# Stacking the high and low token parts into one 512-column product in the feed forward layers of a float32 transformer kernel

## The reference

```
D_FF = 2816
def swiglu(h, w_in, w_out):
    gu = h @ w_in
    return (jax.nn.silu(gu[..., :D_FF]) * gu[..., D_FF:]) @ w_out
```

## Time and profile before

| | |
|---|---|
| time, median of 3 runs | 1937.51 us (1935.63 to 1937.96) |
| the profiled execution: its own time | 1937.2 us |
| its span, first to last instruction | 1935.4 us |
| mean granted TensorE clock | 0.921 of 2.4 GHz |
| PE busy | 1739.7 us, 90% |
| PEld busy | 1601.0 us, 83% |
| DVE busy | 1113.4 us, 58% |
| ACT busy | 887.7 us, 46% |
| POOL busy | 132.5 us, 7% |
| PE's first product of FFN1, of FFN2 | at 368.9, at 611.05 us |

### The profile page before, as it was taken

One profiled execution on the slowest core, in us unless ns is written; L12 is line 12 of the kernel. 1 busy time (PEld: TensorE's weight loads), 2 busy tenths in 40 slices (PEclk: granted clock), 3 DMA queues, 4 the chain that ended last, 5 costly groups with the idle time before them and its releaser, 6 DMA issues.

```text
span 1935.4 us, 27710 instructions
## 1 busy us (share of the span) xinstructions
PE 1739.7 (90%) x11666; PEld 1601.0 (83%) x11666; DVE 1113.4 (58%) x1587; ACT 887.7 (46%) x1365; POOL 132.5 (7%) x197
## 2 busy tenths in 40 slices
PE   7999897699987999978488999889998997999996
PEld 7999795699976998967468999679998886899995
DVE  5555565475555744649455555555555675655554
ACT  5444554344444536430444444544445434444443
POOL 0000000100002012840000000000000000000000
PEclk9999997799998979966588999989999998999998
DMA  7654442255544533520054555445454431445550
GB/s 282 236 195 175 176 156 80 86 201 185 194 174 144 193 119 133 184 77 1 22 195 152 180 183 187 174 155 206 176 195 148 150 108 66 173 169 176 195 189 28
DMA packets 51083, 300.95 MB, mean 155 GB/s; under 512 B 6072, under 2 KB 12688, under 8 KB 17168
## 3 DMA queue, kind: packets, MB, share of 16 engines
q1 hardware_dynamic: 50800, 298.66, 43.2%
q0 software_dynamic: 160, 0.52, 0.1%
HBM read 298.08 MB, written 1.09 MB: 155 GB/s over the span
## 4 chain that ended last, share of the span: by engine, by line
PE 79%; DVE 9%; ACT 7%; issue 2%; POOL 2%; DMA 0%; DVEq 0%; SPq 0%; ACTq 0%; POOLq 0%
PE PS L1740 75%; DVE wlo L1060 1%; ACT wk L643 1%; PE PS L1743 1%; ACT whi L600 1%; POOL st L497 1%; PE PS L1811 1%; DVE wk L1435 1%; DVE SC L1307 1%; DVE wk L1437 1%; DVE X L1137 1%; DVE wk L1439 1%; DVE xn L1145 1%; ACT SC L820 1%; ACT SC L855 1%
## 5 line engine op out<-in xcount | busy, mean ns | idle before, releaser
L1060 DVE TENSOR_TENSOR wlo<-raw,whi 128x1024 fp32r<-128x1024 f32 x528 | 651.2, 1238 | 418.9 <-ACT whi L600 418.1
L1740 PE MATMUL PS<-xhi,whi 128*128 128x256 f32 x2536 | 730.8, 288 | 11.5 <-DVE xlo L1165 8.5
L1740 PE MATMUL PS<-xlo,whi 128*128 128x256 f32 x2536 | 725.3, 286 | 0.0
L1740 PE MATMUL PS<-xhi,wlo 128*128 128x256 f32 x2536 | 724.7, 286 | 0.0
L600 ACT ACTIVATE whi<-raw 128x1024 fp32r<-128x1024 f32 x528 | 551.8, 1054 | 368.5 <-PE PS L1740 368.4
L1740 PEld LDWEIGHTS PS<-xhi,whi 128*128 128x128 f32 x2536 | 494.5, 195 | 20.3 <-DVE xlo L1165 10.9
L1740 PEld LDWEIGHTS PS<-xlo,whi 128*128 128x128 f32 x2536 | 494.8, 195 | 2.1
L1740 PEld LDWEIGHTS PS<-xhi,wlo 128*128 128x128 f32 x2536 | 494.2, 195 | 0.0
L1740 PE MATMUL PS<-whi,hhi 128*128 128x512 f32 x544 | 169.9, 394 | 0.2 <-issue 0.2
L1740 PE MATMUL PS<-wlo,hhi 128*128 128x512 f32 x544 | 168.8, 391 | 0.0
L1740 PE MATMUL PS<-whi,hlo 128*128 128x512 f32 x544 | 168.2, 390 | 0.0
(11 more groups left out here) (252 smaller groups left out, 1539.3 us busy)
## 6 DMA issues: line engine op xcount, KB each, us to landing
raw<-in_w SPq DMA_DIRECT2D x264, 1024.0 KB, 4.8
gr<-in_rows SPq DMA_DIRECT2D x23, 512.0 KB, 3.8
SC<-scratch SPq DMA_DIRECT2D x1, 2048.0 KB, 8.1
SC<-scratch SPq DMA_DIRECT2D x2, 1024.0 KB, 8.5
X<-in_x SPq DMA_DIRECT2D x2, 512.0 KB, 4.4
xn<-in_sc SPq DMA_DIRECT2D x2, 512.0 KB, 7.0
out<-xn SPq DMA_DIRECT2D x2, 512.0 KB, 2.6
SC<-in_pT SPq DMA_DIRECT2D x3, 256.0 KB, 4.2
```

The lines of the kernel that those rows point to most:

```text
L1060: v.tensor_tensor(wlo[:, u % NSPLIT, :], src, hi.bitcast(f32), SUB).then_inc(s_lo, 1)
L1740: return pe.matmul(o, l, r, start=start, stop=stop)
```

## The change

`xhi` and `xlo` become two planes of one tile `xs`, so that for every channel tile k the high and low tokens are 512 adjacent columns. In the feed forward layers `half_unit_both` takes two products for each k: `whi` by the 512 columns (a whole bank), and `wlo` by the 256 high columns added to the bank's first half. The gate and up part each have a bank of their own, out of the same three banks. The two halves of a bank are summed by DVE: two `tensor_reduce` for each f, of 512 elements to 256, into `sg` and `hf`. Silu and the multiplication now read SBUF. Attention and mixer keep `half_unit`.

```diff
-        xhi = sb("xhi", [128, 8, S], f32r)
-        xlo = sb("xlo", [128, 8, S], f32r)
+        xs = sb("xs", [128, 8, 2, S], f32r)
+        xhi, xlo = xs[:, :, 0, :], xs[:, :, 1, :]
...
+        def up_bank(f, i):
+            return 4 + (2 * f + i) % 3
...
(ACT, up(f))
-                    if f == 0:
-                        q.wait_ge(s_sq, n_sq((0, 2, 4, 6, 8, 10)[n], 1))
-                    q.wait_ge(s_used, up_at(n, f) + 2)
-                    if f >= 2:
-                        q.wait_ge(s_hm, F - 1)
-                    b = 4 + f % 3
-                    a.activation(sg[:, f % 2, :], PS[:, b, 0:S], ACT.Silu).then_inc(s_silu, 1)
+                    q.wait_ge(s_gs, F + 1)
+                    a.activation(sg[:, f % 2, :], sg[:, f % 2, :], ACT.Silu).then_inc(s_silu, 1)
...
(DVE, up(f), behind its two half_unit calls)
+                    if f == 0:
+                        q.wait_ge(s_sq, n_sq((0, 2, 4, 6, 8, 10)[n], 1))
+                    else:
+                        q.wait_ge(s_hlo, F - 1)
+                    for i, (d, done) in enumerate(((sg, s_gs), (hf, s_us))):
+                        q.wait_ge(s_used, up_at(n, f) + i + 1)
+                        p = PS[:, up_bank(f, i), :].rearrange("p (a t) -> p t a", a=2)
+                        v.tensor_reduce(d[:, f % 2, :], p, AX.X, ADD).then_inc(done, 1)
                     q.wait_ge(s_silu, F + 1)
-                    if f >= 2:
-                        q.wait_ge(s_hlo, F - 1)
-                    v.tensor_tensor(hf[:, f % 2, :], PS[:, 4 + f % 3, S:2 * S], sg[:, f % 2, :], MUL).then_inc(s_hm, 1)
+                    q.wait_ge(s_us, F + 1)
+                    v.tensor_tensor(hf[:, f % 2, :], hf[:, f % 2, :], sg[:, f % 2, :], MUL).then_inc(s_hm, 1)
...
(PE)
+            def half_unit_both(u, b):
+                hi, lo = (a.rearrange("p (k n) -> p k n", k=8) for a in weight(u))
+                for k in range(8):
+                    mm(PS[:, b, :], hi[:, k, :], xs[:, k, :, :].rearrange("p a t -> p (a t)"), k == 0, k == 7)
+                    e = mm_add(PS[:, b, 0:S], lo[:, k, :], xhi[:, k, :])
+                e.then_inc(s_used, 1)
...
                 def up(f):
-                    b = 4 + f % 3
-                    if f >= 3:
-                        q.wait_ge(s_hm, NF * n + f - 2)
                     if f == 0:
                         q.wait_ge(s_xlo, n_ev(k, 1))
-                    half_unit(up_at(n, f), PS[:, b, 0:S])
+                    if f >= 2:
+                        q.wait_ge(s_us, NF * n + f - 1)
+                    half_unit_both(up_at(n, f), up_bank(f, 0))
                     bg.fill()
-                    half_unit(up_at(n, f) + 1, PS[:, b, S:2 * S])
+                    if f:
+                        q.wait_ge(s_gs, NF * n + f)
+                    half_unit_both(up_at(n, f) + 1, up_bank(f, 1))
                     bg.fill()
```

More of the change, by code:

```diff
@@ L203, in program @@
         s_hi, s_lo, s_used, s_y = (sem(n) for n in ("s_hi", "s_lo", "s_used", "s_y"))
-        s_silu, s_hm, s_hhi, s_hlo = (sem(n) for n in ("s_silu", "s_hm", "s_hhi", "s_hlo"))
+        s_gs, s_us, s_silu, s_hm, s_hhi, s_hlo = (sem(n) for n in ("s_gs", "s_us", "s_silu", "s_hm", "s_hhi", "s_hlo"))
         s_sq, s_yg, s_ms, s_r1, s_X, s_r2, s_xn = (sem(n) for n in ("s_sq", "s_yg", "s_ms", "s_r1", "s_X", "s_r2", "s_xn"))
```

## The result

The changed kernel takes 1948.28 us (median of 4 runs, 1947.55 to 1948.76), beside 1937.74 for the kernel before on the same chip (1935.63 to 1938.22). The ratio is 1.0049, 95% interval 1.0037 to 1.0062: slower by 10.5 us, half a per cent and clear of the noise. The prediction had 1932.

A forecast was written before the change was run, and what follows sets the result against it. PE's pace was taken to bound five of six layers. From 1937.2 us, -18.2 (FFN0, FFN3, FFN4, FFN5), +9.4 (FFN2) and +3.4 (FFN1) gave 1931.8, called 1932; range 1920 to 1952.

The forecast's parts named there:

- the first term of the change: PE, up products: each channel tile falls from 0.360 to 0.3465 us, 27.4 us over all layers.
- the sentence on its bounds: PE: 512- and 256-column products keep their distances side by side, leaving room for no more than a few ns.
- The sign "FFN3 182 us": A check on the forecast: FFN3, a layer without background work, would measure 182 us.
- the last forecast wait: FFN1: f = 7's second half unit waits for the first sum of f = 6, making PE 6.5 us late.
- a granted clock of 1.00 over the stalls: PE at the new stalls in FFN1 and FFN2: the clock would stay at its full level, 1.00.
- The turn: FFN2: one round of DVE's list grows from 5.34 to 6.69 us, against PE's 5.54, so DVE is the bound.
- the table products: FFN2: PE's first table products are released 10.6 us late, by 2.5 + 6 x 1.35.
- the sums read slowly: Rival, DVE: each sum takes 1.04 us instead of 0.69, giving 1951 us; chance 17%.
- the cover: FFN0, FFN3, FFN4, FFN5: DVE hides the sums' 30 us per layer and PE's pace holds; FFN0 may stall 0.3 us.
- All of it arrives: Rival: PE never waits in FFN1 and FFN2, so the full 27.4 us is saved, giving 1910; chance 12%.
- PE saves nothing: Rival: the 13 ns per product belong to something the merge keeps, giving 1955 us; chance 4%.
- The clock falls in the new gaps: Rival: half-clock half units follow three new PE gaps, some 3 us each, giving 1941; chance 12%.

The follow-up runs named there:

- Runs 1 and 2: The changed kernel with only the order of each half unit's products altered: `grouped`, 1936.17 us, and `paired`, 1936.23 us.
- paired: The changed kernel with each half unit's products in the order 512, 256, 256, 512 columns: 1936.23 us, ratio 0.9994 to the kernel before.
- grouped: The changed kernel with each half unit's eight 512-column products first, then its eight 256-column ones: 1936.17 us, ratio 0.9987 to the kernel before.
- Runs 4 and 5: The changed kernel with the old 24 products of 256 columns per half unit, 1957.17 us; and with each sum replaced by a 256-column copy (`short_sum`), 1937.57 us.
- run 7: The changed kernel with a ring of four banks instead of three in FFN1, FFN3 and FFN5: 1949.77 us, ratio 1.0049 to the kernel before.
- hybrid: The new products and sums in FFN0, FFN3, FFN4 and FFN5 alone, FFN1 and FFN2 as in the kernel before: 1929.47 us, ratio 0.9953.
- short_sum: The changed kernel with each sum replaced by a copy of its bank's first 256 columns: 1937.57 us, ratio 0.9993 to the kernel before.

## Why the prediction was wrong

**The step that failed** is the first term of the change: "It now has one of 512 and one of 256: 0.2265 + 0.120 = 0.3465 us", and the sentence on its bounds, "rows 3 show a 512 followed by a 256 and both keep their distances, so I see no room for more than a few ns". Rows 3 show that change once, behind 24 long products. In turn, again and again, the pair is 0.3537 behind the first downs: 6.3 ns saved of 13.5 (6.9 over whole half units). The bound that I left open, "a few ns", was half of the whole saving. FFN0, FFN3, FFN4 and FFN5 give -7.1 instead of -18.2 us, 11 of the 16 us by which the time missed. Runs 1 and 2 show it by changing nothing but the order: with it the four layers give -14.4 and, paired, -16.1. The rest of the 16 is 2.8 in FFN1, 0.3 in FFN2, 1.5 at the start and about 1 outside the layers. (The sign "FFN3 182 us" went by a stretch without the layer's last 2.6 us; as measured here the forecast was 189.0 - 4.6 = 184.4, and FFN3 is 186.6.)

**FFN1** was +6.2 for +3.4. Up to the last forecast wait the step came out: a stall at the fourth half unit, released by the first sum, 3.2 us for the 2.5 predicted, and the second half unit of f = 7 at 430.84, 63.15 us behind the layer's first product where it was 56.32 before. That is 6.8 late for 6.5. I had expected a granted clock of 1.00 over the stalls, and it fell behind the first one. Yet the 1.7 us that this half unit took longer (4.45 for 2.78) cost nothing. Compare `grouped`, where the clock did not fall there, with the changed kernel:

```profile
380.04 2.11 PE L1746 MATMUL PS<-xs,whi 128*128 128x512 f32 x8 [2.39 <-DVE wk L1184]
...
429.55 1.22 PE L1746 MATMUL PS<-xs,whi 128*128 128x512 f32 x2 [2.75 <-DVE wk L1184]
```
```profile
430.84 0.49 PE L1746 MATMUL PS<-xs,whi 128*128 128x512 f32 x1 [2.57 <-DVE wk L1184]
```

From stall to stall there are 49.51 us in `grouped` and 49.52 here (430.84 - 381.32): DVE's list sets the distance, and a slower PE only waits less at its end. The miss stands behind 430.84, where I had 3.1 us given back and 0.6 are. The half units save 0.055 us instead of 0.108 (29 of them, 1.5 us), the wait for a sum at 448.34 costs 0.7, and each pair of downs is 0.03 longer.

**FFN2** was +9.7 for +9.4, with errors that cancel. The turn was right, 6.73 us (634.41 to 641.14) for 6.69. The stall at the fourth half unit is 1.87 us for 3.2, and the table products are 8.4 late for 10.6. Two things make that difference. DVE's background step stood 12.60 us behind the layer's first product before (623.65 - 611.05) and stands 11.26 behind it now. And the first multiply follows that step by 2.00 us (629.08 - 627.08) where it was 0.61: 1.4 later and not 2.5, since the Silu table load does not follow the first sum. ACT's timeline:

```profile
622.19 1.28 ACT L681 ACT_TABLE_LOAD   x1
628.41 0.42 ACT L681 ACTIVATE wk<-wk 128x256 f32<-128x256 f32 x1 [4.93 <-DVE wk L1184]
```

The load runs during the wait and is done 5 us before the sum is. From the table products on the layer loses 1.3 more, where I had 1.2 given back. Most of that stands at one place, where PE waits for ACT's copy of the tables' second products. After:

```profile
752.29 0.66 PE L1991 MATMUL PS<-idt,SC 128*128 128x128 f32 x4 [2.50 <-ACT SC L843]
```
```profile
752.00:757.00 5.00, 4.71 (x20) 4.08 (x21) 2.59 (x2) 1.77 (x3) 4.76 (x4) 0.67 0.31 129
```

The same place before:

```profile
739.35 0.66 PE L1976 MATMUL PS<-idt,SC 128*128 128x128 f32 x4 [1.01 <-ACT SC L844]
```
```profile
739.00:744.00 5.00, 4.65 (x40) 4.65 (x41) 2.66 (x2) 2.49 (x5) 4.76 (x4) 1.00 0.35 144
```

The wait is 1.5 us longer, for which I had 0.7, and the half unit behind it runs mostly at the 1.2 GHz level: 4.42 us for 2.96, another 1.5, which my sum had at nothing. Beside POOL's work, where the earlier trace rows had the split at 1.64 us in the median, it now takes 1.77, and PE waits for DVE 0.17 us once and 0.50 once in the last f.

```profile
L1059 DVE TENSOR_TENSOR wlo<-raw,whi x17: 1219/1774/2312, 795.7 to 843.7; 128x1024 fp32r<-128x1024 f32 x17
```

These waits take up what the half units at 2.82 give back there, 0.055 each and not 0.11.

**DVE's sums** were right: 0.681 us for 0.69. The rival "the sums read slowly" has the sign of the result and not its cause. The rule of the Trainium skill that speaks for it, page "SBUF — State Buffer", section "Door 1: The DMA port swizzle", is stated there for matmuls. Carried over to DVE's reads of PSUM it is not borne out here: 512 elements in pairs 1024 bytes apart take 681 ns, what 512 contiguous ones take in the earlier trace rows (683 and 686). (The slope that the prediction read from the earlier trace rows is (541 - 390) / 224 = 0.67 ns for each element and not 0.69; its upper bound moves by 0.01 us.) Runs 4 and 5 confirm the cover: in the four layers without background work on DVE the sums cost nothing that can be measured.

**The rivals.** "All of it arrives" fell with the first stall. "PE saves nothing" fell too, but was nearer to the four layers than my sum was. "The clock falls in the new gaps" came true three times, at 381, 661 and 753 us, but not at its price of 9 us: the first fall cost nothing, the third 1.5, and behind the second PE waits for DVE and ACT again (1.06 us at 692.13, 2.22 at 700.14). The chance that I gave to slower, 0.30, rested on slow sums; a partial saving on PE with 16 us of loss in two layers beside it was no case of mine.

## What to carry to other kernels

When two pieces of work are merged into one longer instruction, read its price where it will stand among its neighbours; here the same 16 products of a half unit took 2.82 or 2.785 us by their order alone, and that decided between 0.5% slower and no slower (0.9987 and 0.9994 of the time before). Price what the merge puts on another engine by that engine's turn where it is fullest: two sums of 0.68 us were free in four layers and cost 16 to 18 us in two, so the change paid when it was made layer by layer, and in part of a layer. Where one in-order list feeds a consumer with several things, more buffers for one of them (run 7) only name the next one as the releaser.

## What the runs showed of the hardware

- **Two paces for one order of products.** With 512- and 256-column products in turn, each with a weight load of its own, a pair takes 0.3466 us in the opening of FFN0 and FFN3 and 0.3537 behind the first downs. FFN4 and FFN5 begin in the slow pace, FFN1 leaves it behind its 3.23 us stall and falls back behind the first downs. Which pace an opening has differs between profiles with the same products in it: FFN0's is slow (0.353) in `hybrid`, FFN5's is fast (0.347) in `short_sum`. Behind the first downs it is slow in every undisturbed layer with the products in turn. The downs go from 5.47 to 5.50 with it. Grouped or in twos two paces aren't seen. What sets the pace stays open: the granted clock is 1.00 in both, with half the reads of the banks it is the same (run 5), and the fast pace has the sums' load too.
- **The clock behind short stalls.** 3.23, 2.50 and 2.29 us without a product were followed by a half unit mostly at 1.2 GHz, 2.57 us in another place were not. At the place of the 2.50 us the gap is 2.60 in `grouped` and in `paired`; the granted clock behind it was 0.64 and 1.00. The length of the gap alone doesn't decide.
- **A slow half unit can be free.** Where PE next waits for DVE's list, the clock's fall only shortened that wait (49.52 and 49.51 us from stall to stall, with and without it).
- **A table load goes ahead of a wait.** ACT's load for Silu started at 622.19, while the instruction that needs it waited until 628.41.
